# Two attention steps' share of a projection in one run behind the second step, in the dilated mixers of a four-layer decoder trunk

## The chip, the cores and the metric

The kernel runs on one core of a Trainium2 chip. The metric is the device time of one execution in microseconds, median over several runs. TensorE (PE) does the matmuls, VectorE (DVE), ScalarE (ACT) and GpSimd (POOL) do the elementwise work, SyncE (SP) issues the loads of the weights. Every engine runs its own instructions in their written order; they wait for each other on counting semaphores.

## The reference, cut to what matters

Four layers of a decoder trunk on 512 tokens of width 1024: a token mixer (layers 0 and 3: dilated window attention; 1: sparse attention; 2: gated DeltaNet), then a squared-ReLU MLP. The change touches the dilated mixer alone:

```python
qkv = (h @ w_in).reshape(B, S, 3, A_N_GROUPS, A_HEADS, HEAD_DIM)   # 3 groups, 8 heads of 64
q = rms_norm(qkv[:, :, 0], q_gain)
k = rms_norm(qkv[:, :, 1], k_gain)
v = qkv[:, :, 2]
for g, (window, dilation) in enumerate(((128, 1), (512, 4), (2048, 16))):
    o, lse = dilated_window_attention(q[:, :, g], k[:, :, g], v[:, :, g], bias, window, dilation)
wts = softmax(stack(lses), axis=0)
y = sum(wts[..., None] * stack(outs), axis=0) @ w_out
```

All is float32. The matmuls with weights are made of three passes of a shorter format: weight and activation are each split into a high and a low part, and high x high, high x low and low x high are added.

## The kernel before, in words

**Weights.** They come in chunks of 128 x 2048 numbers, two buffers deep. For each chunk SP loads raw (`chunk`, L477; it waits for `w_lo_done` of the chunk two before), ACT rounds it to w_hi (`rounding`, L717), POOL subtracts to get w_lo (`split`, L571; in the mixer in four pieces of two columns each, spread over three attention steps by `share`), PE multiplies.

**The dilated mixer** has four pairs of heads. The queries and keys of pair 0 and all values are projected first. Those of pairs 1 to 3 are 18 tiles (9 chunks with a query tile and a key tile each) of 24 matmuls, 432 matmuls in all. They are the fill: PE does them between the pieces of attention of the pairs before.

**Attention steps.** There are 32 units, 8 per pair: four of the near window (`z` 0 to 3) and four of the two dilated groups. A loop over steps `s` runs on every engine. On PE (the loop at L1989) step `s` is: `weigh(s-3)` (probabilities times values, L1959), `scores(s)` (L1920 near, L1927 far), `turn(s-2)` (transposes of probabilities, L1943), then `fill(2*s)` and `fill(2*s + 1)` (L1895), then early parts of the output projection from step 26 on (`joined`, L1778), then at `z == 1` `difference(f-1)` (L1973), which spreads log-sums of a finished pair. Each `fill(G)` does the matmuls lo to hi that `a_share(G)` gives (L435), and then `sum_qk` (L1865) for each tile that ended in half-step G-1: one matmul that sums the squares of a head. `sum_qk` waits for DVE's addition of epsilon and for ACT's Ln of the tile before (one PSUM bank for the sums).

**The other engines in step s.** DVE: `inverses(s-1)`, `outputs(s-3)` (L1288), `logits(s)` (L1269, two halves), `part(2*s)`, at `z == 3` `mixed(f-1)` (L1307, L1310, L1312), the copy of the turned probabilities of unit s-2 (L1353; from unit 24 on ACT does it, L933), `part(2*s + 1)`. DVE's `part(G)` is `add_eps` (L1246) for each tile that ended in half-step G. ACT: at `z == 1` the six loads of the next pair's bias (`load_pair_bias`, L862), `probs(s)` (L900), at `z == 2` three operations on the log-sums (L936 to L940), `part(2*s)`, `part(2*s + 1)`. ACT's `part(G)` is `qk_rms` (Ln L850, Exp L852) for the tiles that ended in G-1, then `qk` (Square L825, copy L826) and the rounding of the next but one chunk for the tiles that ended in G. POOL: `weights_scaled(s-1)` (L594), pieces of splits, `part` with `qk_scale` (L583) for the tiles that ended in G-1, more pieces of splits. All take the half-steps in which tiles end from `a_ended`, and that from `a_share`, so the orders of all engines move with it.

The single buffers matter here: one tile for the squares, so that `qk_tile` waits:

```python
mem = {0: dict(sq=[asq], rs=ars), 1: dict(sq=bsq, rs=brs)}
...
elif Q - q_base(kind) >= len(sqs) or (Q and len(sqs) == 1):
    act.wait_ge(ssq_done, Q - len(sqs) + 1)
```

and one tile `ars` for the inverse root, so that the Ln of a tile waits for POOL's scaling of the tile before (`act.wait_ge(qk_ready, Q)`). `A_FILL` is 52: two half-steps in each of 26 steps.

Of the kernel before, what the change touches and what calls it, by code (L numbers as in the profile page):

```python
# [46 lines left out]
A_FILL = 52  # L47
# [51 lines left out]
def trunk(nc, x_in, rel_bias, params, c_gates, masks, bucket_rows, bias_mask, mlp_w1, mlp_w2,  # L99
# [20 lines left out]
    with ExitStack() as ctx:  # L120
# [314 lines left out]
        def a_share(G):  # L435

            total = 24 * 6 * (A_PAIRS - 1)
            return min(total, total * G // A_FILL), min(total, total * (G + 1) // A_FILL)

        def a_tiles(i):  # L440

# [3 lines left out]
        def a_ended(i, G):  # L445

            lo, hi = a_share(G)
            return [x for j, x in enumerate(a_tiles(i)) if lo < 24 * j + 24 <= hi] if G >= 0 else []
# [1249 lines left out]
        def _(pe):  # L1698
# [168 lines left out]
            def mixer_a(li, i):  # L1867
# [27 lines left out]
                def fill(G):  # L1895

                    lo, hi = a_share(G)
                    for j, (k, n, t) in enumerate(a_tiles(i)):
                        a, b = max(lo, 24 * j), min(hi, 24 * j + 24)
                        if a < b:  # L1900
                            tile(n, t, a - 24 * j, b - 24 * j)
                    for k, n, t in a_ended(i, G - 1):
                        sum_qk(0, a_q(i, k, n, t))
# [460 lines left out]
```

## Time and profile before

| what | value |
|---|---|
| median of 3 runs | 2822.63 us (2821.99 to 2824.24) |
| the profiled execution | 2823.16 us |
| its span | 2821.3 us |
| PE busy | 2734.3 us (97%) |
| DVE, ACT, POOL busy | 1043.5, 1082.1, 1385.4 us |
| mean granted TensorE clock | 0.99 |

Busy time is the share of the span in which an engine executes; PE's weight loads (PEld) overlap its matmuls. The chain that ended last is followed back from the last instruction, at each step to what released it.

### The profile page before, as it was taken

How to read it: one execution, taken by the hardware profiler on the slowest of the kernel's cores; microseconds unless marked ns; L12 is line 12 of the kernel's file. 1: busy time of each engine (PE TensorE's matmuls, PEld its weight loads, DVE VectorE, ACT ScalarE, POOL GpSimd, SP SyncE). 2: the span in 40 equal slices, each digit the busy share in tenths (PEclk: the TensorE clock that was granted, in tenths of full speed). 3: DMA queues.
4: the chain of work that ended last, by engine and by line, in shares of the span. 5: the costliest groups of instructions: out<-in, count | busy, mean ns of one | idle time of the engine just before them, and what ended most of it. 6: DMA issues, size and time to landing. Idle time of an engine off the chain costs nothing.

```text
span 2821.3 us, 37261 instructions
## 1 busy us (share of the span) xinstructions
PE 2734.3 (97%) x14594; PEld 2190.6 (78%) x14594; DVE 1043.5 (37%) x1936; ACT 1082.1 (38%) x1638; POOL 1385.4 (49%) x1074
## 2 busy tenths in 40 slices
PE   7999899999989999999999998999999999899999
PEld 5977678888766788887777776888888977688887
DVE  4035422113486512213677774311123044522112
ACT  4355543224346433324334333422234355533221
POOL 3567544445446344455343442444545466544443
PEclk8999999999999999999999999999999999999999
DMA  4331123233422133224211110323223422132232
GB/s 125 103 77 53 45 91 104 90 104 89 105 45 69 55 102 97 97 89 113 61 46 46 46 46 16 102 93 105 89 96 90 112 53 68 46 100 94 89 104 74
DMA packets 271884, 227.82 MB, mean 81 GB/s; under 512 B 29204, under 2 KB 259348, under 8 KB 271748
## 3 DMA queue, kind: packets, MB, share of 16 engines
q1 hardware_dynamic: 260880, 216.29, 25.3%
q10 hardware_dynamic: 10868, 9.66, 1.5%
q8 instruction: 93, 1.52, 0.2%
q14 instruction: 43, 0.35, 0.0%
HBM read 223.62 MB, written 2.30 MB: 80 GB/s over the span
## 4 chain that ended last, share of the span: by engine, by line
PE 88%; DVE 5%; ACT 3%; POOL 2%; issue 1%; DMA 0%; ACTq 0%; DVEq 0%; POOLq 0%
PE bank L1824 49%; PE bank L1733 18%; PE bank L1890 5%; PE bank L2117 2%; PE bank L2206 2%; PE bank L1865 1%; PE bank L1943 1%; PE bank L1778 1%; PE bank L1959 1%; POOL w_lo L571 1%; PE bank L1927 1%; POOL arena L638 1%; ACT w_hi L717 1%; PE bank L1973 1%; PE bank L1920 1%
## 5 line engine op out<-in xcount | busy, mean ns | idle before, releaser
L571 POOL TENSOR_TENSOR w_lo<-raw,w_hi 128x512 fp32r<-128x512 f32 x808 | 1076.4, 1362 | 1180.2 <-ACT w_hi L717 1180.2
L717 ACT ACTIVATE w_hi<-raw 128x2048 fp32r<-128x2048 f32 x202 | 385.6, 1909 | 456.9 <-PE bank L1824 423.3
L1824 PE MATMUL bank<-h_hi,w_hi 128*128 128x512 f32 x1024 | 400.8, 391 | 0.0
L1824 PE MATMUL bank<-h_hi,w_lo 128*128 128x512 f32 x1024 | 398.4, 389 | 0.0
L1824 PE MATMUL bank<-h_lo,w_hi 128*128 128x512 f32 x1024 | 398.4, 389 | 0.0
L1824 PE MATMUL bank<-g_hi,w_hi 128*128 128x512 f32 x1024 | 398.3, 389 | 0.0
L1824 PE MATMUL bank<-g_lo,w_hi 128*128 128x512 f32 x1024 | 398.3, 389 | 0.0
L1824 PE MATMUL bank<-g_hi,w_lo 128*128 128x512 f32 x1024 | 398.3, 389 | 0.0
L1733 PE MATMUL bank<-h_hi,w_hi 128*128 128x512 f32 x776 | 319.8, 412 | 7.2 <-POOL w_lo L571 7.2
L1733 PE MATMUL bank<-h_lo,w_hi 128*128 128x512 f32 x776 | 314.3, 405 | 0.0
L1733 PE MATMUL bank<-h_hi,w_lo 128*128 128x512 f32 x776 | 312.2, 402 | 0.0
L770 ACT ACTIVATE arena<-arena 128x512 f32<-128x512 f32 x128 | 80.9, 632 | 425.9 <-DVE arena L1213 425.9
L1213 DVE SCALAR_TENSOR_TENSOR arena<-bank,rs 128x512 f32<-128x512 f32 x128 | 88.5, 692 | 372.7 <-PE bank L1824 349.2
L1228 DVE TENSOR_TENSOR x<-x,bank 128x512 f32<-128x512 f32 x96 | 66.0, 688 | 431.5 <-PE bank L1824 431.5
L1824 PEld LDWEIGHTS bank<-h_lo,w_hi 128*128 128x128 f32 x1024 | 192.2, 188 | 41.2 <-issue 1.4
L1824 PEld LDWEIGHTS bank<-h_hi,w_hi 128*128 128x128 f32 x1024 | 192.2, 188 | 41.1 <-issue 1.4
L1824 PEld LDWEIGHTS bank<-h_hi,w_lo 128*128 128x128 f32 x1024 | 192.2, 188 | 40.0
L1824 PEld LDWEIGHTS bank<-g_lo,w_hi 128*128 128x128 f32 x1024 | 192.2, 188 | 40.0
L1824 PEld LDWEIGHTS bank<-g_hi,w_lo 128*128 128x128 f32 x1024 | 192.2, 188 | 39.9
L1824 PEld LDWEIGHTS bank<-g_hi,w_hi 128*128 128x128 f32 x1024 | 192.2, 188 | 39.8
L1733 PEld LDWEIGHTS bank<-h_hi,w_hi 128*128 128x128 f32 x776 | 148.0, 191 | 43.2 <-POOL w_lo L571 9.0
L1733 PEld LDWEIGHTS bank<-h_lo,w_hi 128*128 128x128 f32 x776 | 147.8, 190 | 34.2 <-issue 6.7
(265 smaller groups left out, 3829.9 us busy)
## 6 DMA issues: line engine op xcount, KB each, us to landing
raw<-in_mlp_w SPq DMA_DIRECT2D x128, 1024.0 KB, 5.2
raw<-in_a_w_in SPq DMA_DIRECT2D x48, 512.0 KB, 5.1
raw<-in_c_w_in SPq DMA_DIRECT2D x32, 512.0 KB, 5.5
raw<-in_a_w_in SPq DMA_DIRECT2D x12, 1024.0 KB, 5.1
raw<-in_b_w_in SPq DMA_DIRECT2D x18, 256.0 KB, 4.1
raw<-in_a_w_out SPq DMA_DIRECT2D x4, 1024.0 KB, 4.9
raw<-in_b_w_in SPq DMA_DIRECT2D x4, 1024.0 KB, 5.4
arena<-bias_scratch ACTq DMA_DIRECT2D x16, 256.0 KB, 3.5
```

What stands on the lines that cost most here:

```text
L571: ins = nc.gpsimd.tensor_tensor(w_lo[s][:, k, :], raw[s][:, k, :], w_hi[s][:, k, :].bitcast(F32), ALU.subtract)
L638: nc.gpsimd.tensor_tensor(btm[t % 2][:, :, 0:n], bbias[f % 2][:, :, TOK - n:TOK], score[b].unsqueeze(1).to_broadcast([P, 2, n]), ALU.add). ...
L717: nc.scalar.activation(w_hi[s][:], raw[s][:], ACT.Copy).then_inc(w_hi_done, 1)
L770: nc.scalar.activation(gsq[j % 2], relu_t[j % 2], ACT.Square).then_inc(gsq_done, 1)
L1213: nc.vector.scalar_tensor_tensor(relu_t[j % 2], lin_bank[j % 2][:], 0.0, rs, ALU.max, ALU.mult).then_inc(relu_done, 1)
L1228: nc.vector.tensor_tensor(x[:, c, :], x[:, c, :], lin_bank[c % 2][:], ALU.add).then_inc(x_added, 1)
L1733: mm = nc.tensor.matmul(o, lhsT, rhs, start=start, stop=stop)
L1778: mm = nc.tensor.matmul(lin_bank[t % 2][:], w[(n0 + f // 2) % 2][:].rearrange("p k n -> p (k n)")[:, c:c + P], a[:, f, :], start=k == 0, s ...
L1824: mm = nc.tensor.matmul(lin_bank[j][:], w[s][:, c, P * j:P * j + P], a[:, c, :], start=c + z == 0, stop=c == CT - 1 and z == 2)
L1890: mm = nc.tensor.matmul(bank[2 + b][:], keys, quads[w][:, c, :], start=half + c + z == 0, stop=half == 1 and c == 3 and z == 2)
L2117: mm = nc.tensor.matmul(out[z:z + HD], lhsT[:, z:z + HD], rhs, start=start, stop=stop)
L2206: mm = nc.tensor.matmul(bk4(3)[:, c, :], atl[k % 3][:, c, :], Tm[:, c, :], start=True, stop=True)
```

## The change

`a_share` gives other shares of the 432 matmuls to the half-steps. Before, each of half-steps 0 to 51 got 8 or 9. Now a half-step gets something only if it is 1, 5, 9, ..., 53, the second one of an even step: up to 16, 49, 83, 116, 149, 182, 216, 249, 282, 315, 348, 382, 415 and 432 matmuls in total. Odd steps do attention alone (and sums). Everything else is as it was.

```diff
@@ -435,7 +435,8 @@
         def a_share(G):
 
             total = 24 * 6 * (A_PAIRS - 1)
-            return min(total, total * G // A_FILL), min(total, total * (G + 1) // A_FILL)
+            run = (G + 2) // 4 * 4 - 2
+            return tuple(max(0, min(total, total * g // A_FILL)) for g in (run, run + 4 if G % 4 == 1 else run))
```

## Rows read from the trace of the kernel before

**Rows 1.** The page: busy time, the chain by engine, loads of this mixer's weights.

```profile
PE 2734.3 (97%) x14594; PEld 2190.6 (78%) x14594; DVE 1043.5 (37%) x1936; ACT 1082.1 (38%) x1638; POOL 1385.4 (49%) x1074
...
PE 88%; DVE 5%; ACT 3%; POOL 2%; issue 1%; DMA 0%; ACTq 0%; DVEq 0%; POOLq 0%
...
raw<-in_a_w_in SPq DMA_DIRECT2D x48, 512.0 KB, 5.1
```

**Rows 2.** Stretches of steps 0 to 26: length, then PE, PEld, DVE, ACT, POOL busy, clock.

```profile
145.00:305.70 160.70, 158.86 (x971) 116.30 (x971) 71.93 (x208) 88.92 (x190) 113.81 (x103) 1.00 0.25 66
2248.00:2409.00 161.00, 159.12 (x971) 116.56 (x972) 72.29 (x209) 88.92 (x190) 114.04 (x104) 1.00 0.25 67
```

**Rows 3.** Timeline of step 7, layer 0: start us, length us, engine, line, operation.

```profile
180.28 0.42 PEld L1959 LDWEIGHTS bank<-arena 128*64 128x64 f32 x8 [0.35 <-issue]
...
180.87 0.71 PE L1927 MATMUL bank<-arena 64*128 64x128 f32 x8
...
181.93 0.48 PE L1733 MATMUL bank<-h_hi,w_lo 128*128 128x512 f32 x1
...
182.21 0.51 ACT L900 ACTIVATE arena<-arena 128x256 f32<-128x256 f32 x1 [2.38 <-DVE arena L1269]
...
182.44 0.08 DVE L1269 DVE_READ_ACCUMULATOR2_ANT arena<- 128x1 f32 x1
...
183.21 0.57 ACT L825 ACTIVATE sq<-bank 128x512 f32<-128x512 f32 x1
...
183.82 1.13 DVE L1246 TENSOR_TENSOR sq<-sq,em 128x512 f32<-128x512 f32 x1 [1.30 <-ACT sq L825]
...
185.66 1.02 PE L1865 MATMUL bank<-sq,com 128*128 128x512 f32 x2
186.61 0.66 PE L1959 MATMUL bank<-arena 128*64 128x128 f32 x8
...
186.72 0.60 ACT L850 ACTIVATE sq<-bank 128x512 f32<-128x512 f32 x1 [2.35 <-PE bank L1865]
```

**Rows 4.** Groups by form, 145 to 306: busy us, mean ns, idle before them.

```profile
L571 POOL TENSOR_TENSOR w_lo<-raw,w_hi 128x512 fp32r<-128x512 f32 x37 | 49.1, 1336 | 21.4 <-ACT w_hi L717 21.4
L594 POOL TENSOR_SCALAR arena<-arena 128x256 f32<-128x256 f32 x42 | 41.6, 1003 | 3.5 <-DVE arena L1278 3.5
L583 POOL TENSOR_TENSOR arena<-arena,sq 128x512 f32<-128x512 f32 x17 | 21.8, 1284 | 29.4 <-ACT sq L852 29.4
...
L717 ACT ACTIVATE w_hi<-raw 128x2048 fp32r<-128x2048 f32 x9 | 17.2, 1911 | 0.0
...
L1246 DVE TENSOR_TENSOR sq<-sq,em 128x512 f32<-128x512 f32 x18 | 20.1, 1119 | 39.2 <-ACT sq L825 39.2
```

**Rows 5.** Timeline of step 11 (with `mixed`) to the start of step 12.

```profile
207.71 0.44 PE L1959 MATMUL bank<-arena 128*64 128x128 f32 x4
...
212.71 0.68 DVE L1353 COPY arena<-bank 128x512 f32<-128x512 f32 x1
...
213.44 0.66 PE L1959 MATMUL bank<-arena 128*64 128x128 f32 x8 [0.17 <-DVE arena L1353]
```

**Rows 6.** Timeline at step 17, ACT's queue: the bias loads of a pair.

```profile
243.71 2.74 ACTq L862 DMA_DIRECT2D arena<-bias_scratch  x6
```

**Rows 7.** Waits of PE, 306 to 346 (steps 27 on): total, times, longest.

```profile
PE bank L1943 <- POOL arena L594: 2.4, 1, 2.4
PE bank L1959 <- ACT arena L933: 2.0, 2, 1.3
```

**Rows 8.** Timeline of PE in layer 2, behind its longest wait there.

```profile
1712.60 1.11 PE L2195 MATMUL bank<-com,arena 128*128 128x128 f32 x4 [5.25 <-DVE arena L1619]
```

**Rows 9.** Stretches as in rows 2 (third number from the right is the granted clock).

```profile
316.00:317.00 1.00, 0.81 (x4) 0.71 (x4) 0.00 (x0) 0.00 (x0) 1.00 (x2) 0.50 0.00 0
1712.00:1714.00 2.00, 1.40 (x6) 1.25 (x6) 2.00 (x3) 0.25 (x1) 2.00 (x2) 0.50 1.07 379
...
1716.00:1718.00 2.00, 1.74 (x20) 1.23 (x20) 0.00 (x0) 0.60 (x1) 1.27 (x1) 0.50 0.00 0
1752.00:1754.00 2.00, 1.99 (x6) 1.22 (x5) 1.83 (x3) 1.44 (x3) 0.00 (x0) 0.56 0.00 0
```

## The prediction

> **What bounds the kernel now.** I read the page first: PE is busy for 97% of the span and the chain that ended last is 88% PE [rows 1]. The reader is to see that only PE time, or a new PE wait, can move the end. Then the two stretches that the change touches, by engine: attention steps 0 to 26 of layers 0 and 3, 160.7 and 161 us long, with PE busy for all but 1.84 and 1.88 us of them [rows 2]. So today nearly everything else in these steps is hidden behind PE. The timeline of one ordinary step shows why [rows 3]: weigh, scores and turn take 1.65 us of PE (180.28 to 181.93), then its 16 projection matmuls (it is step 7, 116 to 132 of 432) run for 3.7 us (181.93 to 185.66) while DVE and ACT deal with the scores. The profiled execution took 2823.16 us (span 2821.3), 0.5 us over the median of 2822.63; the sum is made against the former and moved by this half microsecond. About 0.2%, 5.6 us, is what a measurement can tell from no change.
>
> **What the change does.** a_share maps the 52 half-steps on runs: half-step 1 gets matmuls 0 to 16, half-step 5 gets 16 to 49, and so on, about 33 behind every even step and none behind the odd ones; the last 17 go behind step 26 instead of 25. The number of matmuls, bytes and evictions is the same. What is removed: 13 pairs of entries into the projection. Coming out of the projection, the weight load of weigh has an idle 0.35 us ahead of it [rows 3], where the steady spacing of matmuls is 3.7/16 = 0.23. I take 0.2 us per odd step for the way out and in, 13 x 0.2 = 2.6 us per layer (bounds 0 and 0.35 each). What is added is the lost cover of each odd step.
>
> **An odd step with nothing special.** Count from the start of weigh(s-3). PE is done after 1.65 us; the row-sum matmul of a tile that ended in the run before takes 0.95 more (185.66 to 186.61) [rows 3], so 2.6. DVE ends both logits 2.24 after the start (182.44+0.08) and then copies the turned weights, 0.68 [rows 5], so the next weigh can start at 2.95: stall 0.35. Steps 5, 7, 15, 21 and 23 are of this kind: 1.75 us. Step 1 has no sum and no copy; scores(2) waits for logits(1): 1.65 from the start of the scores against 0.65 of PE: 1.0. Step 11 (and 19) has mixed() on DVE before the copy: weigh to weigh took 213.44 - 207.71 = 5.73 us [rows 5], bound by DVE already, and PE will have 2.6 us of work in it: step 11 stalls 3.1. In step 17 the difference must wait for the Ln of its tile, which stands behind probs on ACT: 3.03 + 0.6 = 3.7 against 2.6: 1.1.
>
> **Runs in which two tiles end.** Tiles end at multiples of 24 and runs at 16, 49, 83, 116, 149, 182, 216, 249, 282, 315, 348, 382, 415, 432. Five runs end two: (24,48), (120,144), (192,216), (288,312), (384,408), before the odd steps 3, 9, 13, 19 and 25. Before, no half-step ended two. There is one buffer for the squares (asq) and qk_tile waits on ACT for the sum of every earlier tile; PE does that sum only in the next half-step that has a fill call, now behind the attention part of the odd step. Behind ACT's wait are its rounding, probs(s) and the first Ln; behind DVE's wait in add_eps are outputs and logits(s). Chain, from the start of the odd step: sum of the first tile at 1.65; ACT's Square 1.06 later (185.66 to 186.72), 2.7; DVE's add 0.61 later (183.21 to 183.82), 3.3, and 1.12 long [rows 3, 4], 4.45; reciprocal and output copy, 4.95; first logits, 5.35; probs 1.1 (ACT went from them at 182.21 to the next work at 183.21), 6.45; Ln of the first tile 0.6, 7.05; only then the second sum on PE, which ends at 8.0. Without waits that is 3.55. Stall 4.5 us for step 13. Step 3 has ACT's rounding of 1.91 [rows 4] in the chain, partly beside DVE: 4.9. Step 19 adds mixed() and the copy behind logits (5.8 + 3.0 + 0.68): 5.95. Steps 9 and 25 also have difference(), which waits for the second Ln, and that for POOL's scaling of the first tile (ars is single): in step 25 POOL does two weights of 1.0 or less, a split of 1.34 and the scaling of 1.28 [rows 4], ends at 9.0, Ln 9.65: 6.15. Step 9 has the rounding and the six bias DMAs on ACT's queue, 2.74 us [rows 6], in front of probs, and the split behind the rounding on POOL: 11.55 against 3.55, 8.0. Sum of the five: 4.5+4.9+5.95+6.15+8.0 = 29.5 (bounds 20, if the pieces overlap, and 40, if POOL and DVE slow each other).
>
> **The end of the fill.** Tile 17 now ends in step 26, its scaling on POOL in step 27 stands behind two splits, and scores(28) waits for it (about 8.1 us behind the start of step 27, PE is there at 5). Today the wait at step 28 is another: turn behind POOL 2.4 and weigh behind ACT 2.0 us [rows 7]. One takes the place of the other; I count +1 (bounds -1 and +4). SP: loads of the next but one chunk go out when its raw buffer is split, well over two steps before ACT needs them, at 160.7/27 = 6 us a step, against 5.1 us to landing [rows 1]: cost 0, hidden by those steps; without that cover up to one landing time.
>
> **The clock.** An idle PE costs twice. After the wait of 5.25 us that ended at 1712.6 [rows 8] the granted clock is 0.50 until 1718 [rows 9], the lower of its levels (1.2 of 2.4 GHz), so 5.4 us of work at half rate, 2.7 lost; in another place it is 0.56 over 2 us, 0.9 lost. I take 2.5 for each of the five double steps and 1.5 for step 11 (between the two places): 14 us per layer (bounds 0, if it holds, and 25, if every odd step pays some 2). The Trainium skill (TensorE: Matmul & The Clock Gate, Why this matters for your kernels) wants no idle gaps between bursts of matmuls because the clock falls back in them. By this rule the trace agrees. The same page of the Trainium skill (Loop structure matters more than you think) favours long dense runs of matmuls, which is what the change makes; by that alone it would bring something (case d below). The rows show a full clock in these stretches now, 1.00 [rows 2], so a denser run has no clock left to gain.
>
> **Sum per layer**: 1.75 + 1.0 + 3.1 + 1.1 + 29.5 + 1.0 = 37.5; less the waits that exist already, 1.9 [rows 2], and the entries 2.6: 33.0; clock 14: 47. Two layers: 94. 2823.2 + 94 = 2917.2 for the profiled execution, 2917 for the median.
>
> **Rivals.** (a) The waits come but the clock holds, since attention matmuls lie within them: 2822.6 + 66 = 2889. For: the longest single idle in a double step is some 4.4 us, not 5.25. Against: step 28, where idle stretches of 1.3 and 2.4 us already brought 0.50 [rows 7, 9]. Chance 0.18. (b) The double steps cost little more than single ones, because ACT and DVE get to the blocked work sooner than my chain: per layer 13 x 0.35 + 3 x 2 for mixed + 1.1 + 1, less 4.5, and no clock: 12.65 - 4.5 = 8.15, so 2839. Against it stands the program order on ACT. Chance 0.08. (c) POOL falls behind: in 145 to 306 it is busy 113.8 of 160.7 us [rows 2], splits come in a lump behind each run, weights_scaled stands behind them, and turn waits for it in even steps too; with 1.3 us (one split) in each of 13 pairs, twice, plus clock: 2917 + 34 + about 10 = 2961. Chance 0.08. (d) Other side, faster: place, the hand-over from odd to even step. If DVE's logits and copy are done by the time PE is through with its sum, i.e. within 2.6 us instead of 2.95, and ACT's Square of the second tile is not held up, then all that is left is the entries, 2.6, and the waits that go, 1.9: 2 x 4.5 = 9, 2814. It would decide if 0.35 us could be found in each odd step and no run ended two tiles; the second is contradicted by the list above. Chance 0.03. (e) The new mapping comes out as the old in effect (PE gets the same work per 11 us and the queues absorb the shift): 2823. Chance 0.02, since odd steps plainly have no matmul left.
>
> **Numbers.** Forecast case 0.61, centred on 2917, itself 2890 to 2945 by the bounds on the double steps (-9.5, +10.5 per layer) and the clock. The range 2868 to 2946 takes in (a) and leaves out (b), (c), (d), (e) and the tails. Faster 0.03, same 0.02, slower 0.95.
>
> **What would show it.** In the profile of the changed kernel: L1865 on PE waits some 4 us for ACT or DVE in each of the steps 3, 9, 13, 19, 25 (ten times in all), ACT's Square (L825) idles behind L1865, weigh (L1959) waits for DVE's copy about 0.3 us in plain odd steps and 3 us in step 11, difference (L1973) waits for L850 in 9, 17 and 25, and the granted clock of 145 to 340 falls to about 0.9. PE's waits in the two mixers grow from 2 to some 35 us each. I am wrong if L1865 does not wait, if turn (L1943) behind POOL carries the loss (then c), or if the clock in these stretches stays at 1.00 with the waits there (then a). The Trainium skill (SBUF, Who interferes with whom) says that a DVE operation with two inputs in SBUF and a GpSimd one that reads there block each other. The trace has the same add at 1.13 us [rows 3] and 1.12 in the mean [rows 4] and does not show it alone; if lumps on POOL stretch it, the double steps go towards 40.

## The result and the profile after

The changed kernel takes 2925.3 us, the median of 4 runs (2923.77 to 2926.47), against 2823.43 for the kernel before in the same set (2821.99 to 2827.24). The ratio is 1.0358 [1.0343, 1.0372]: 102 us slower. The profiled execution took 2923.77 us (span 2922.0), which is 100.6 us over the one before. In the changed kernel every line behind 438 stands one higher.

The page of the changed kernel, busy time by engine and the chain that ended last by engine:

```profile
PE 2769.1 (95%) x14594; PEld 2211.9 (76%) x14594; DVE 1046.3 (36%) x1936; ACT 1080.5 (37%) x1638; POOL 1378.2 (47%) x1074
...
PE 85%; DVE 5%; ACT 4%; POOL 3%; issue 2%; DMA 0%; ACTq 0%; DVEq 0%; POOLq 0%
```

The work is the same (the counts of [rows 1]). PE's busy time has grown by 35 us although it does the same 14594 instructions, so some of them ran at the lower clock. The other 66 us of the span are time in which PE does nothing. The same stretch of both mixers, the attention of the kernel after (columns as in [rows 2]):

```profile
139.00:395.00 256.00, 215.25 (x1224) 155.80 (x1222) 93.51 (x269) 108.78 (x240) 131.10 (x122) 0.89 0.19 49
...
2290.00:2550.00 260.00, 218.30 (x1235) 158.75 (x1235) 94.15 (x270) 109.96 (x241) 131.13 (x122) 0.89 0.19 51
```

And the kernel before over the stretch that answers to the first of them:

```profile
139.00:345.00 206.00, 198.82 (x1228) 146.04 (x1227) 91.61 (x269) 109.11 (x240) 134.66 (x122) 0.98 0.24 63
```

Layer 0 needs 50 us more for the same work. DVE, ACT and POOL did nearly the same amount. PE was idle for 41 us of 256 instead of 7 of 206, and its clock was 0.89 instead of 0.98. Added up in slices of 1 us, the granted clock stood at 0.50 for 54.6 us of this stretch (a slice between 0.50 and 1.00 counts in proportion, and a part of these us lies within the waits), and for 6.8 before. The text calls this half clock. What PE waited for in 139 to 395 (us in total, times, longest):

```profile
PE bank L1866 <- issue: 12.7, 3, 4.8
PE bank L1866 <- ACT sq L851: 9.9, 2, 5.3
PE bank L1960 <- DVE arena L1354: 4.1, 3, 2.3
PE bank L1974 <- ACT sq L851: 3.5, 3, 1.8
PE bank L1928 <- POOL arena L584: 3.3, 1, 3.3
PE bank L1944 <- POOL arena L595: 3.2, 2, 2.9
PE bank L1960 <- ACT arena L934: 1.2, 1, 1.2
PE bank L1921 <- DVE arena L1270: 0.9, 1, 0.9
```

The reader is to see five waits of the row-sum matmul (L1866, 22.6 us in all), where the kernel before had one, of 0.9. Over the whole run there are ten, 44.6 us.

Now where the time lies. From weigh to weigh in PE's timeline of layer 0, over an odd step and the even one behind it (both kernels do the same work in such a pair), in us:

| steps | before | after | more |
|---|---|---|---|
| 3, 4 | 12.91 | 19.82 | 6.91 |
| 5, 6 | 12.06 | 12.24 | 0.18 |
| 7, 8 | 11.83 | 12.02 | 0.19 |
| 9, 10 | 15.60 | 24.39 | 8.79 |
| 11, 12 | 12.31 | 15.81 | 3.50 |
| 13, 14 | 12.93 | 20.30 | 7.37 |
| 15, 16 | 11.84 | 12.34 | 0.50 |
| 17, 18 | 14.40 | 14.46 | 0.06 |
| 19, 20 | 12.69 | 20.14 | 7.45 |
| 21, 22 | 12.28 | 13.40 | 1.12 |
| 23, 24 | 11.83 | 12.02 | 0.19 |
| 25, 26 | 12.14 | 21.07 | 8.93 |
| 27, 28 | 9.86 | 11.00 | 1.14 |

With 3.28 us ahead of step 3 the table comes to 49.6 us; twice that is 99 of the 100.6. (Counted from the first scores, which began 1.03 us earlier in the changed kernel, step 3 is 4.3 us late; layer 3 has 4.3 as well.) The five pairs with a run in which two tiles end hold 39.45 of the 49.6. Three of the plain ones cost 0.2 each.

A plain odd step, 5, in PE's timeline of the kernel after (start us, length us, engine, line, operation):

```profile
178.41 0.66 PE L1960 MATMUL bank<-arena 128*64 128x128 f32 x8
...
181.31 0.44 PE L1960 MATMUL bank<-arena 128*64 128x128 f32 x4
```

It is over in 2.90 us without any cover. Step 13, where the run before it ended two tiles:

```profile
242.87 0.66 PE L1960 MATMUL bank<-arena 128*64 128x128 f32 x8
...
244.60 1.02 PE L1866 MATMUL bank<-sq,com 128*128 128x512 f32 x2
245.72 0.60 ACT L826 ACTIVATE sq<-bank 128x512 f32<-128x512 f32 x1 [5.20 <-PE bank L1866]
...
246.35 1.09 DVE L1247 TENSOR_TENSOR sq<-sq,em 128x512 f32<-128x512 f32 x1 [7.48 <-ACT sq L826]
...
247.44 0.69 DVE L1317 TENSOR_TENSOR g_lo<-arena,g_hi 128x512 fp32r<-128x512 f32 x1
...
248.77 0.51 ACT L901 ACTIVATE arena<-arena 128x256 f32<-128x256 f32 x1 [1.36 <-DVE arena L1270]
...
249.77 0.57 ACT L851 ACTIVATE sq<-bank 128x512 f32<-128x512 f32 x1
...
250.45 2.05 PE L1866 MATMUL bank<-sq,com 128*128 128x512 f32 x2 [4.83 <-issue]
```

This is the chain. ACT had idled for 5.20 us in front of the Square of the second tile (L826), because the one buffer still held the squares of the first; DVE had idled for 7.48 in front of its add behind it. Logits stand behind the add, probs (L901) behind the logits, the Ln of the first tile (L851) behind probs, and only then can PE sum the second tile, 4.83 us late. That sum, 2.05 long instead of 1.02, already runs at half clock. The profile names this wait "issue" and not by a releaser; what ended last before it is the Ln, at 250.34.

### The profile page after: what moved, and what is told of

Same layout as the page of the kernel before. It is cut to its first block, busy times and chain, and to the rows that moved or that the text cites. A ratio compares the mean times of both kernels' runs of the same rounds, so it can differ in the third digit from the quotient of the medians.

```text
span 2922.0 us, 37261 instructions
## 1 busy us (share of the span) xinstructions
PE 2769.1 (95%) x14594; PEld 2211.9 (76%) x14594; DVE 1046.3 (36%) x1936; ACT 1080.5 (37%) x1638; POOL 1378.2 (47%) x1074
## 4 chain that ended last, share of the span: by engine, by line
PE 85%; DVE 5%; ACT 4%; POOL 3%; issue 2%; DMA 0%; ACTq 0%; DVEq 0%; POOLq 0%
PE bank L1825 48%; PE bank L1734 18%; PE bank L1891 5%; PE bank L2118 2%; PE bank L2207 2%; POOL w_lo L572 1%; PE bank L1960 1%; ACT w_hi L718 1%; PE bank L1779 1%; PE bank L1944 1%; PE bank L1866 1%; PE bank L1928 1%; PE bank L1974 1%; POOL arena L639 1%; PE bank L1760 1%
```

## The experiments

The theory: the loss is the ends of two tiles in one run, through the single buffer and the order on ACT and DVE, and the lower clock behind each wait. The rival: it is the lost cover of the odd steps, whatever ends in them. All kernels below are compared with the kernel before in the same sets (medians 2821.83 to 2824.08). Where no other base is named, the edit is to the changed kernel.

**A second buffer for the squares.**

```diff
+        asq2 = part(TOK)
...
+            if kind == 0:
+                return asq2 if Q not in opening and Q % 2 else asq
...
+                elif kind == 0:
+                    act.wait_ge(ssq_done, Q if Q - 1 in opening else Q - 1)
...
```

> The changed kernel with a second buffer for the squares of the fill's tiles, so that ACT's Square of the second tile of a run no longer waits for the first tile's sum. Theory (the five runs per layer in which two tiles end cost through that single buffer, 39.5 of 49.6 us per layer): the second sum then waits for the first Ln alone, behind probs, about 1.1 us instead of 4.7 to 5.3 us; with a shorter time at the lower clock that is 5 to 6 us less in each of ten places, 2870 us (2860 to 2885). Rival A (the loss is the cover that odd steps lack, whatever ends in the run): 2915 us or more, with the waits moved to weigh and turn. Rival B (POOL's lumps of splits): turn's waits behind POOL grow and the time is 2895 or more.

Measured: 2887.41 us, 1.0227 [1.0197, 1.0256]; 38 us of the 102 are gone, and 17 us more than expected are left. The five double pairs cost 3.64, 4.60, 3.39, 5.11 and 4.18 us over before instead of 6.9 to 8.9. PE's waits in 139 to 385:

```profile
PE bank L1969 <- DVE arena L1363: 5.8, 3, 2.4
PE bank L1983 <- ACT sq L860: 5.4, 3, 2.9
PE bank L1875 <- issue: 3.8, 3, 2.1
...
PE bank L1875 <- ACT sq L860: 3.0, 2, 1.9
```

The sum (here L1875) now waits 6.8 us instead of 22.6, but some of it has moved on: the next weigh behind DVE's copy (L1969, 5.8 from 4.1) and the difference behind the Ln (L1983, 5.4 from 3.5). The buffer is one link of the chain, not the whole.

**One end a run.** The same runs behind the even steps, but where a run would end two tiles it stops one matmul short of the second end; the 1 to 8 matmuls left are done behind the odd step's attention. The odd steps are as bare as before.

```diff
+            run = (G + 2) // 4 * 4 - 2
+            a, b, c = (max(0, min(total, total * g // A_FILL)) for g in (run - 4, run, run + 4))
+
+            def cut(lo, hi):
+                return 24 * (hi // 24) - 1 if hi // 24 - lo // 24 > 1 else hi
+
+            if G % 4 == 1:
+                return b, cut(b, c)
+            if G % 4 == 3:
+                return cut(a, b), b
+            return (cut(a, b),) * 2 if G % 4 == 2 else (b, b)
```

> The changed kernel, but the five runs in which two tiles end stop one matmul short of the second end; the 1 to 8 matmuls that are left go behind the odd step's attention. All other runs as in the change. Theory (two ends in one run are the cost): the second sum moves one step on and its Square starts after the first sum anyway, so of some 7 to 9 us per place 1.5 to 3 are left: 2870 us (2855 to 2885). Rival A (odd steps without the fill's cover are the cost): only 1 to 8 matmuls of cover come back, 0.2 to 1.9 us each, 2905 us or more.

Measured: 2864.30 us, 1.0145 [1.0115, 1.0174]; 61 of the 102 are gone. Half clock falls from 54.6 to 23.9 us a layer. Steps 5 to 10 (two plain pairs and a former double one) take 38.64 us against 39.49 before. PE's waits in 139 to 370:

```profile
PE bank L1969 <- DVE arena L1363: 7.3, 3, 3.4
...
PE bank L1875 <- DVE sq L1256: 2.7, 2, 1.7
```

So the theory holds for the largest part, and the rival is left with some 40 us. They lie at the start (4.4 us a layer), in (11, 12) with 3.9 and in 17 to 20 with 5.2, where DVE has mixed(), and in (3, 4), (13, 14) and (25, 26) with 1.7, 2.2 and 1.8.

**Does the clock follow the wait?** 16 matmuls that nobody reads are put ahead of the second sum, in the ten places. The kernel computes the same outputs; it does 160 matmuls more.

```diff
-                    for k, n, t in a_ended(i, G - 1):
+                    for x, (k, n, t) in enumerate(a_ended(i, G - 1)):
+                        for _ in range(16 * x):
+                            nc.tensor.matmul(bank[4 + (G // 2 + 1) % 2][:], halves_r[:], h_hi[:, 0, :], start=True, stop=True)
```

> The changed kernel with 16 matmuls of 512 columns (3.7 us at the full clock), whose result nobody reads, ahead of the second sum in each of the ten places where two tiles ended, in a PSUM bank that is free there. The wait for the second sum is nearly the same in length, but PE works in it. Theory (part of the loss is TensorE's lower clock behind the idle stretch): the granted clock stays at 1.00 behind them, and some 2.5 us per place go, 2900 us (2890 to 2908). Rival (the waits alone): 2925 us, within 5.

Measured: 2915.57 us, 1.0326 [1.0296, 1.0356]: 10 us less than the changed kernel where 25 were expected. First the clock at step 13 in both. The changed kernel (third number from the right is the granted clock):

```profile
248.00:249.00 1.00, 0.00 (x0) 0.00 (x0) 1.00 (x6) 0.23 (x1) 0.69 (x1) 0.87 0.00 0
252.00:253.00 1.00, 1.00 (x7) 0.58 (x8) 0.00 (x0) 0.32 (x1) 0.59 (x1) 0.50 0.00 0
```

With the unread matmuls:

```profile
251.00:252.00 1.00, 1.00 (x4) 0.24 (x6) 0.00 (x0) 0.46 (x1) 1.00 (x2) 1.00 0.00 0
253.00:254.00 1.00, 1.00 (x11) 0.83 (x9) 0.61 (x3) 0.82 (x2) 0.05 (x1) 1.00 0.00 0
```

So the clock does follow the wait, and does not fall here once PE is kept at work; half clock is 32.2 us a layer instead of 54.6. But most of what a faster PE gains it gives back, because it comes too early for others: PE waits 10.6 us for POOL's w_lo over the whole run against 7.2, and in (9, 10) its wait for the difference grows to 3.03 us (from 1.84). The pair takes 25.33, 0.94 more than without the filler. (3, 4) and (13, 14) gain 2.0 and 1.2.

**The Ln first.** In the double places the Ln and Exp of the first tile are put ahead of probs on ACT.

```diff
-                    for k, n, t in a_ended(i, G - 1):
+                    for k, n, t in a_ended(i, G - 1)[-1:]:
...
+                    for k, n, t in a_ended(i, G)[:-1]:
+                        qk_rms(0, a_q(i, k, n, t))
```

> The changed kernel with one step moved in ACT's order: in the five double places the Ln and Exp of the first tile come directly behind the Square, copy and rounding of the second one, ahead of probs of the odd step. Theory (the second sum waits for the first Ln, and that stands behind logits and probs): its wait falls from 4.7 to about 2.3 us in steps 13, 19 and 25 and by less in steps 3 and 9, where the rounding stays in front; 2895 us (2880 to 2908). Rival (it is DVE's addition of epsilon that the sum waits for): the same time as the change, 2925 us, within 5, and the wait is put down to DVE.

Measured: 2920.36 us, 1.0343 [1.0313, 1.0373]: 5 us less, 30 expected. PE's waits over the whole run:

```profile
PE bank L1962 <- DVE arena L1356: 18.3, 9, 3.2
...
PE bank L1976 <- ACT sq L851: 15.0, 6, 3.5
```

In six of the ten places the sum now waits for DVE's add, at most 1.9 us (in the other four for up to 4.0), but weigh behind DVE's copy doubles (8.7 us in the changed kernel, 18.3 here), and so does the difference (7.3, 15.0). Probs and logits were pushed back by what the Ln gained, and the next weigh needs them. It is the rival of the expectation that came: the time is within 5 us of 2925, and the wait stands at DVE's add.

**Both together**, the second buffer and the Ln first.

> Both of the edits: a second buffer for the squares, and the Ln and Exp of the first tile ahead of probs. Alone they gave 2887 and 2920 us. Theory (the second sum waits for two things in one chain, the Square behind the first sum and the Ln behind probs; what is taken from one only shows the other, and DVE's copy): with both gone its wait is 0.7 us in steps 3, 13 and 19, and with it goes the lower clock there; 2870 us (2860 to 2878), more than the two alone would add to (2882). Rival (the edits add up or overlap): 2880 us or more.

Measured: 2890.60 us, 1.0242 [1.0222, 1.0263], nothing beyond the second buffer alone. Of PE's waits in 139 to 385 the sum's are down to 3.9 us, and the loss stands at weigh behind DVE's copy (8.2 us, against 5.8 with the buffer alone) and at the difference (5.8). Neither of these orders takes the loss away; moving the ends apart took the largest part of it.

**Covering what is left.** To "one end a run", the old shares again in steps 0 to 2, 10 to 12 and 18 to 20 (bare: 3, 5, 7, 9, 13, 15, 17, 21, 23, 25):

```diff
+A_ALONE = (3, 5, 7, 9, 13, 15, 17, 21, 23, 25)
...
+            if s in A_ALONE:
+                hi = old(2 * s)
+                left = cut(old(2 * s - 4), hi) if s - 2 in A_ALONE else hi
+                return (left, hi) if second else (left, left)
+            if s - 1 in A_ALONE:
+                lo, hi = old(2 * s - 2), old(2 * s + 2)
+                return (lo, cut(lo, hi)) if second else (lo, lo)
...
+            return old(G), old(G + 1)
```

> The kernel with one tile end a run (2864 us), and besides the old even shares around steps 0 to 2, 10 to 12 and 18 to 20; ten odd steps per layer are still attention alone. Theory (what was left there, 20 us per layer, sits in three places: turn of unit 0 behind POOL's splits in steps 1 and 2, and DVE's mixed() without cover in steps 11 and 19; plain odd steps cost next to nothing): some 4.5 + 4 + 4.5 us per layer go, 2838 us (2832 to 2846). Rival (every odd step without cover costs about the same, 20/13 = 1.5 us): three of 13 steps go, 2855 us.

Measured: 2864.99 us, 1.0151 [1.0131, 1.0172]: no gain, 27 expected. Against "one end a run" the start gives 5.3 us a layer (4.5, if counted from the first scores) and (11, 12) 3.3, and other pairs take nearly all of it back: (3, 4) 1.2, (13, 14) 1.5, (19, 20) 2.0 and (21, 22) 2.5. The expectation took this for a test of the cover alone, but the old shares also move the ends. The run behind step 18 stops at 311, and the half-step right behind it ends the tile at 312: with its cover back (19, 20) takes 20.67 us, more than with a bare step 19 (18.71) and than before (12.69). What (11, 12) gives back, 3.3 us, is the price of lost cover in step 11.

**Plain odd steps alone** (`A_ALONE = (3, 5, 13, 15, 21)`, else the old shares).

> The old even shares, but in steps 3, 5, 13, 15 and 21 of each layer attention alone with the share in one run behind the step after; each run ends one tile and none of these steps has difference() or mixed(). Theory (such a pair costs the 0.35 us that DVE's copy is late less the 0.2 us of one entry, 0.15 to 0.2 us as measured in steps 5 to 8 of the change): +1.5 to 3 us in ten places, 2825.5 us, no difference that can be told. Rival (lost cover costs wherever it is lost): 1 us or more each, 2834 us or more. Other rival (one run instead of two shares pays, by the entries): below 2822 us.

Measured: 2873.95 us (4 runs), 1.0186 [1.0169, 1.0203], 48 us over the expectation. Of the bare pairs (5, 6) and (15, 16) cost 0.2 and 0.5 as in the changed kernel, but (3, 4) costs 3.07, (13, 14) 1.45 and (21, 22) 3.64. In (3, 4) the turn of step 4 waits 1.95 us for POOL, and in (13, 14) the sum and the next weigh wait 1.0 each for DVE; in both a tile ends in the last half-step before the bare step. In (21, 22) no end is near (336 in half-step 40, 360 in 45), and weigh waits 2.97 us:

```profile
288.09 1.34 DVE L1334 TENSOR_TENSOR g_lo<-arena,g_hi 128x512 fp32r<-128x512 f32 x1 [3.42 <-ACT g_hi L963]
...
291.03 1.12 PE L1977 MATMUL bank<-arena 128*64 128x128 f32 x8 [2.97 <-DVE arena L1371]
```

The low part of the mixed output (`g_lo`), which DVE makes at the end of steps 12 and 20 behind ACT's high part, stands ahead of the logits of steps 13 and 21, and so of the copy for which weigh waits. Before, the share of step 21 covered this. So this rival is right for three of the five bare pairs, with 8 of some 22 us a layer. The surprise is in steps with cover: (7, 8) takes 18.31 us against 11.83, (17, 18) 17.15 against 14.40, (23, 24) 16.34 against 11.83. Step 7 there:

```profile
186.91 1.02 PE L1883 MATMUL bank<-sq,com 128*128 128x512 f32 x2
...
187.97 0.60 ACT L868 ACTIVATE sq<-bank 128x512 f32<-128x512 f32 x1 [1.60 <-PE bank L1883]
...
189.14 0.58 ACT L843 ACTIVATE sq<-bank 128x512 f32<-128x512 f32 x1
...
189.31 1.27 POOL L601 TENSOR_TENSOR arena<-arena,sq 128x512 f32<-128x512 f32 x1 [2.97 <-ACT sq L870]
...
189.75 1.77 DVE L1264 TENSOR_TENSOR sq<-sq,em 128x512 f32<-128x512 f32 x1 [4.17 <-ACT sq L843]
...
191.58 1.72 PE L1883 MATMUL bank<-sq,com 128*128 128x512 f32 x2 [1.82 <-DVE sq L1264]
```

The run behind step 6 ends a tile (96 matmuls), and the old share of step 7 ends the next one (120) in the half-step right behind. No half-step ends two, and yet the chain is there: sum, Ln, Exp, Square (L843), add, sum. PE waits another 1.67 us for POOL's w_lo in step 8. The other two of these pairs have ends in neighbouring half-steps as well (264 and 288, 360 and 384). The even share was never only cover: 24 matmuls at 8 or 9 a half-step keep the ends three half-steps apart (two in two places).

**Bare steps with the ends kept apart.** `A_ALONE = (5, 7, 9)`: here no two ends come close.

> The old even shares, but in steps 5, 7 and 9 of each layer attention alone, with one run behind each of steps 6, 8 and 10, stopped short of a second tile's end as in the kernel with one tile end a run. Here no tile ends at the end of the step before a bare one with old shares around it, and no two ends are closer than two half-steps. Theory (a bare odd step is free where tile ends stay apart; the 50 us of the plain pairs came from ends that fell close together): steps 5 to 10 took 38.6 us in the kernel with one tile end a run against 39.5 before, steps 11 and 12 lose some 0.6 at the return to the old shares: 2822 us within 3, no difference that can be told. Rival (bare odd steps cost in themselves, five of them 50 us and so three 30): 2850 us.

Measured: 2823.32 us (11 runs) against 2822.78 (15 runs), 1.0001 [0.9992, 1.0010]. PE's waits in 139 to 345 (the rest are 2.0 and 0.8, as in the kernel before):

```profile
PE bank L1961 <- POOL arena L612: 2.8, 2, 2.4
...
PE bank L1977 <- DVE arena L1371: 1.0, 1, 1.0
```

Two bare odd steps a layer and one (9, with the bias loads and the difference) with only 6 matmuls behind its attention cost nothing that the runs can tell (about 3 us for all six). This is the plainest answer to the rival: lost cover by itself costs nothing in steps of this kind. It does cost in the steps where DVE or POOL has more to do: 3.3 us in step 11 with mixed() and 3.6 in step 21 with `g_lo`, as above, and some 4 in step 1.

**The start alone**: "one end a run" with the old shares in steps 0 to 2.

> The kernel with one tile end a run (2864 us), with the old even shares in steps 0 to 2. Theory (turn of unit 0 waits for POOL behind the splits of the last value chunk, and only step 1's share covers that): 5.3 us per layer come back at step 3, but the second tile now ends right before the bare step 3 and turn in step 4 waits 2 us for POOL, as in the kernel with covered places: net 4 per layer, 2856 us (2853 to 2860). Rival: the whole 5.3 per layer stays, 2853 us or less; or nothing, 2864.

Measured: 2860.02 us (2855.41 and 2864.63), 1.0130 [1.0112, 1.0149]. The two runs lie too far apart to give the size; in the profiled one, the slower, step 3 begins 3.5 us earlier (14.62 us behind the first scores, as before the change, against 19.12: 4.5) and (3, 4) takes 1.4 more.

**Towards a better kernel.** Three attempts to beat the kernel before, all from the old even shares: a fill that ends a step earlier (`A_FILL = 50`), the old shares up to half-step 40 and then 10 a half-step, and the latter with steps 5, 7 and 9 bare. The first of these:

> The kernel before the change with A_FILL 50 instead of 52: shares of 8.64 instead of 8.3 matmuls, so that the fill ends a step earlier and POOL has the last tile's scaling and the last splits behind it before step 28, where PE waits 2.4 us for it now. If that wait and the lower clock behind it are due to this lump: up to 3 us per layer less, against one bare step 25 at 0.35 to 1.5: 2817 to 2821 us. If tile ends at other places cost (the spacing becomes 2.8 half-steps): 2824 us or more.

Measured: 2834.04 us (5 runs), 1.0038 [1.0025, 1.0052]. The end gets faster as meant, since no tile is late for step 28 (3.55 us against 5.53), but PE's waits over the whole run show what the denser shares bring: for w_lo 11.1 us in 4 waits, against 7.2 in 2 before. The new one in step 13 is 1.98 us long. The profiled execution is the fastest of the five (2829.84), so it shows less than the typical loss. The second:

> The kernel before the change with the old even shares up to half-step 40 and 10 matmuls in each half-step from there, so that the fill ends at half-step 49 instead of 51. With A_FILL 50 steps 25 to 29 took 20.5 us against 27.0 with 17 matmuls (3.9 us) in them before, 2.6 us per layer less, but the denser shares of the earlier steps brought waits behind POOL's splits that cost more. Theory (only the end pays, the density costs): 2817.5 us within 2. Rival (10 matmuls a half-step bring the same waits in the last ten half-steps): 2823 us or more.

Measured: 2833.84 us (5 runs), 1.0037 [1.0024, 1.0051], with the same loss in one place, a wait for w_lo of 2.95 us in step 22. The third:

> The same end, and besides bare steps 5, 7 and 9 with runs behind 6, 8 and 10 as in the spaced kernel, whose profile showed steps 5 to 12 about 0.9 us shorter per layer. Theory: 1 to 2 us below the kernel with the early end alone, 2816 us. Rival: the same as that kernel.

Measured: 2840.33 us (5 runs, 2829.83 to 2840.71), 1.0060 [1.0046, 1.0073]. Its profiled execution was the one of 2829.83, so where the typical ones lose is not shown. Nothing found here beats the kernel before.

## Why the prediction was right, and where it was off

Forecast 2917, measured 2925.3, inside the range of 2868 to 2946, and the likeliest case is the one that came. By its own steps:

- **Plain odd steps**, 0.35 less 0.2 for the entries: 0.15 forecast; 0.18, 0.19 and 0.19 measured in the pairs (5, 6), (7, 8) and (23, 24). Right. (15, 16) had 0.50, with a wait of 0.28 for POOL in it. In (21, 22) came 1.12, which was not forecast. The prediction counted step 21 among the plain ones and left out `g_lo`, 1.35 us on DVE ahead of the logits:

```profile
311.02 1.35 DVE L1317 TENSOR_TENSOR g_lo<-arena,g_hi 128x512 fp32r<-128x512 f32 x1 [2.20 <-ACT g_hi L946]
...
313.97 0.66 PE L1960 MATMUL bank<-arena 128*64 128x128 f32 x8 [1.12 <-DVE arena L1354]
```

- **Two tiles in a run**, the five places. Waits forecast 29.5; measured in the waits for sum, difference and weigh 4.68 (step 3), 5.27 + 1.84 (9), 4.83 (13), 3.73 + 0.73 (19), 4.14 + 0.78 (25), 26.0 in all. In step 13 the chain up to the second sum was to take 7.05 us from the start of the step and took 7.58 (242.87 to 250.45); the missed link is DVE's L1317 of 0.69 (`g_lo` again), which stands between the add and the logits. The waits of steps 9, 19 and 25 were forecast too large by 0.9, 1.5 and 1.2. In 9 and 25 the chain itself was not shorter: the difference began 11.89 and 9.70 us from the start of the step, forecast were 11.55 and 9.65. But PE's second sum within it took 2.05 us at half clock instead of 1.02, so that a part of the stall appears as slow work and not as a wait. In step 9 two errors cancel: the bias loads were counted as 2.74 us ahead of probs and cost 0.2 (last section), and the rest of the chain took that much more, of it 1.27 for a second split on POOL (211.24) ahead of the first tile's scaling. Step 19 was in truth shorter, 8.71 to the next weigh against 9.5. With 12.5 of clock, less 1.0 for the entries and 0.9 for a wait that existed, 40.1 were forecast for these pairs and 39.45 measured. That "one end a run" takes away 61 of the 102 us shows the mechanism; the second buffer shows its first link (38 us).
- **Step 11**: 3.1 + 1.5 of clock, less 0.2 and an old wait of 0.17, made 4.2; 3.50 measured. Weigh waited 2.27 us for DVE's copy, as forecast the only wait there.
- **Step 17**: 1.1, less 0.2 and the old wait of 0.78 for the difference, made 0.1; 0.06 measured.
- **Steps 0 to 2**: 1.0 less 0.2 forecast, 3.28 measured at the start of step 3 (4.3, if one counts that the first scores began at 139.65 instead of 140.68). This is the term that was mis-sized most. It looked at scores(2) behind logits(1), and that wait is there (0.9); what it missed is on POOL. The start in POOL's timeline, and PE's turn of step 2:

```profile
142.90 4.97 POOL L572 TENSOR_TENSOR w_lo<-raw,w_hi 128x512 fp32r<-128x512 f32 x4 [7.36 <-ACT w_hi L718]
147.84 3.00 POOL L595 TENSOR_SCALAR arena<-arena 128x128 f32<-128x128 f32 x4
```

```profile
149.09 0.44 PE L1944 MATMUL bank<-com,arena 128*128 128x128 f32 x2 [2.89 <-POOL arena L595]
```

  The last value chunk's split, 5 us in four operations on end, stands ahead of the first weights to be scaled. Before, step 1's share of the projection covered that; with a bare step 1 PE waits 2.89 us. With the start covered again the turn does not wait, and step 3 begins as early as before, counted from the first scores.
- **The end of the fill**: +1 forecast, +1.14 measured. The wait is the one named, scores(28) behind POOL's scaling (3.3 us), in place of turn behind POOL (2.4) and a part of weigh behind ACT (2.0 before, 1.2 now).
- **The clock**: 14 us a layer forecast. What the five double pairs grew beyond their waits is 39.45 - 26.0 + 1.0 + 0.9 = 15.3 and in (11, 12) 3.50 - 2.27 + 0.37 = 1.6, so 17: 3 more, where the waits were 3.5 fewer. (This is a remainder and holds all that is not a wait; PE's busy time in layer 0 grew by 16.4, from 198.82 to 215.25.) Forecast granted clock "about 0.9" in the stretch, measured 0.89. Of rival (a), the clock that holds, nothing is left.
- **POOL falling behind in even steps** (rival c): turn waits for POOL only in step 2 and for 0.28 us in step 16. The add of a tile beside POOL, from which the prediction feared more, did not add to the double steps (last section). The mean of 1.12 in [rows 4], from which it read the add's length, mixes adds of 0.7 us, of 1.1 to 1.2 and, beside splits, of 2.05 and 2.17.
- **PE's waits**: "some 35" us a mixer, measured 38.8 in layer 0.

Term by term, forecast and measured, in us a layer: doubles 40.1 and 39.45; step 11 4.2 and 3.50; step 17 0.1 and 0.06; the other plain pairs 0.75 and 2.18; the start 0.8 and 3.28; the end 1.0 and 1.14. That makes 47 and 49.6. Of the 8 us between 2917 and 2925.3 this difference gives 5.3 in two layers (the start and step 21, less what step 11 and the doubles were too high), 1.4 lie outside the table, and 1.5 is the median above the profiled execution. The total is closer than its terms: shorter waits in the doubles and more at the start cancel in part, and that is luck.

What the prediction did not see is how little each link is worth by itself. Nine of the twelve expectations for the runs were missed, all on the hopeful side, by 13 to 48 us. For the second buffer and the Ln first the profile shows the wait that was taken away one link further; with the covered places and the plain pairs it shows tile ends that the edit had moved, and lost cover in step 21.

## What to carry to other kernels

Filler matmuls spread evenly through a loop do two things: they cover PE's waits, and they space the ends of the tiles, behind each of which hangs a chain through ACT, DVE and POOL. Before moving such work into lumps, list which tiles end in which slot; here two ends in one slot cost 7 to 9 us each, in neighbouring slots 3 to 8. Bare steps without them cost nothing where the other engines have little to do (5, 7, 9), and 1 to 4 us where DVE or POOL has an extra piece ahead of what PE needs next (1, 11, 21). So list these pieces too. Where one engine holds the chain in program order, a second buffer or another order moves the wait to the next link; take away the coincidence rather than the link, and read the next consumer's wait before counting a gain.

## What was unexpected

**Waits of 1.8 to 2.9 us can be enough for the lower clock.** The prediction rested on a wait of 5.25 us and on two close ones of 1.3 and 2.4 [rows 7 to 9]. In the changed kernel the granted clock is at 0.50 from 150 to 153 us, behind the wait of 2.89 us in step 2 (one of 0.88 is 3.6 us ahead of it), and from 232 to 235 behind the single wait of 2.27 for weigh(12). In step 7 of the plain-pairs kernel it is at 0.50 from 192 to 195 behind a wait of 1.82, and in step 13 of the kernel with the second buffer it stays at 1.00 behind one of 2.08 (242.30). A slice of each, plain pairs first, then second buffer:

```profile
192.00:193.00 1.00, 1.00 (x2) 0.00 (x0) 0.20 (x2) 0.00 (x0) 0.00 (x0) 0.50 0.00 0
```

```profile
243.00:244.00 1.00, 1.00 (x11) 0.50 (x10) 0.00 (x0) 0.00 (x0) 1.00 (x2) 1.00 0.00 0
```

So the length of a wait doesn't decide it alone; what does is not shown. A single wait less than half as long as that of [rows 8] can cost some 3 us at half rate on top, by estimate 1.5 of them lost. And since the filler removes the spells behind the second sums and gives back only 10 us of the run, what the clock costs can't be won back by itself.

**Loads issued on ACT's queue cost ACT nearly nothing here.** Step 9 of the changed kernel, ACT and its queue:

```profile
206.86 1.91 ACT L718 ACTIVATE w_hi<-raw 128x2048 fp32r<-128x2048 f32 x1
207.01 1.90 ACTq L863 DMA_DIRECT2D arena<-bias_scratch  x4
208.96 0.51 ACT L901 ACTIVATE arena<-arena 128x256 f32<-128x256 f32 x1 [0.19 <-issue]
```

The loads stand between the rounding and probs in ACT's program, are issued while the rounding runs, and probs comes 0.19 us behind it. This is one place; no run varies the loads.

**DVE's add and POOL stretch each other.** In step 7 of the plain-pairs kernel, above, the add took 1.77 us beside POOL's two-input scaling (L601), which had begun 0.44 us ahead of it; with POOL idle such an add takes 1.09 (246.35 in the changed kernel, above). The kernel before has it too, which the prediction overlooked. POOL's two scalings beside the add of [rows 3] there, and another place:

```profile
183.03 0.93 POOL L594 TENSOR_SCALAR arena<-arena 128x256 f32<-128x256 f32 x1
...
183.93 1.83 POOL L594 TENSOR_SCALAR arena<-arena 128x256 f32<-128x256 f32 x1
...
220.67 1.27 POOL L571 TENSOR_TENSOR w_lo<-raw,w_hi 128x512 fp32r<-128x512 f32 x1
220.76 2.17 DVE L1246 TENSOR_TENSOR sq<-sq,em 128x512 f32<-128x512 f32 x1 [4.48 <-ACT sq L825]
```

In the second place the add begins 0.09 us behind a split and takes 2.17, while the split keeps its 1.27. In the first the add (183.82, 1.13 long) begins when the first scaling is nearly done and keeps its length; the second scaling begins 0.11 us behind the add and takes 1.83 us instead of 0.93. The Trainium skill (SBUF — State Buffer, Who interferes with whom) says that a DVE operation with two inputs in SBUF and a GpSimd one that reads there contend for a shared port, and that the one which comes second is held up. By this rule the trace agrees in both places, with the caution that POOL's lengths are rough. It doesn't agree in size everywhere: in the changed kernel an add of this kind that begins 0.12 us behind a scaling (329.93, 0.93 long) takes 1.31 (330.05) and not 1.9. The prediction had named this as a possible addition; in the changed kernel's first mixer the add is never over 1.31 us, so it was next to none there. In the plain-pairs kernel it is 0.7 of each wait of 1.8, and in step 13, where the add takes 2.13 beside a split, all of the wait of 1.03.
